# Index scores by four row groups, norm sums dealt between products, and another place for the inner parts

## The chip, the cores and the metric

The kernel runs on one NeuronCore of a Trainium2 chip. The metric is the device time of one execution in microseconds (us). Three runs of the kernel before gave 1913.39, 1914.81 and 1916.36, so the median is 1914.81 us.

## What is computed

The reference is two transformer blocks over 512 tokens of width 1024, in float32. The first block has two layers. Each takes an RMS norm, one wide projection that is split into 19 parts, four groups of heads (latent attention A, differential attention B, sparse attention C, a short convolution D), gates, and an output projection. The second block is a feed-forward (inner width 2816), a mixer with 16 heads, cross attention to 256 memory tokens, and a second feed-forward. What the change touches is this:

```python
# group C: which 128 keys a query may see
score = relu(einsum('bqhd,bkd->bqhk', qi, kidx))      # 8 index heads of 32
index = einsum('bqh,bqhk->bqk', wi, score) * idx_scale
_, sel = lax.top_k(index, topk)                       # topk = 128
# group A: latents are normed before they are projected up
q  = _rmsnorm(cq, qa_g) @ w_uq                        # cq 256 wide
kv = _rmsnorm(ckv, kva_g) @ w_ukv                     # ckv 128 wide
# second block
x = x + 0.5 * swiglu(rms_norm(x, g_ffn1), w_ffn1_gu, w_ffn1_down)
```

## The kernel before, in words

**Products.** Activations stand transposed, features on partitions: `hhi`, `hlo` (input of a projection, high and low part), 8 chunks of 512 tokens, 2048 bytes a chunk. Each float32 product is three fast ones (`products`, L859): input high by weight high, low by high, high by low. A *job* is one block of 128 output columns: 8 chunks of three products into one of two PSUM banks (`proj`), then evicted by DVE. Weights come by DMA in slots of a ring of four. For each slot ACT makes the high part (`make_high`, L1430), and POOL or DVE the low part (`make_low`, L652 or L1785): POOL for the jobs of a layer, DVE for the second block's feed-forward. A slot is prepared when the job two before it has ended.

**A layer.** The order of the work on PE is written out by hand: jobs QI0, QI1 (index queries), KI (index keys, copied four times over the partitions), KR, CQ0, then the four of `IDX_JOBS` (CQ1, CKV, BQ0, BK0), then VT0, the spreading of the latents' roots, and 34 steps of attention (L1072, L1084, L1108) that are filled with further jobs by a table. The output jobs OUT0 to OUT7 end the layer.

**Index scores.** There are 8 heads by 3 query blocks (the first block needs none), 24 units a layer. A query block sees 256, 384 or 512 keys, so that is the width of a unit. `idx_pair` (L951) does two units at once: for each of three passes (high by high, high by low, low by high) it issues one matmul of 32 rows for each of two heads, which stand on two different groups of 32 partitions, into `score[0]` and `score[1]`. A pair stands after chunks 0, 3 and 6 of each of the four jobs (`IDX_CHUNKS`), 12 pairs a layer. ACT takes each unit through relu into one of four buffers (L1529), DVE multiplies it by the head's weight and adds it to `index` (L1928, L1931). A pair waits until the relus of the pair before it are done.

**Topk.** 32 half rounds on DVE (`topk_half`: 8 largest values of three rows, or taking them out of the rows) find the 128 largest. The first four come before VT0 is evicted, the other 28 are dealt over the first 22 attention steps.

**Latent norm.** ACT squares the three latents (L1520), one in each of the first three jobs of `IDX_JOBS`. After BK0, PE sums the squares over partitions by 4 matmuls with one column for each latent (`add_squares`, L829; each shows as two instructions in the trace). DVE makes means, POOL the roots (L647), DVE diagonals of them (L1811), and PE spreads them over the partitions (`spread_roots`, L843). DVE then scales the latents (L1973) and takes the row minima of attention step 0 (L1829).

**Norm of a large input.** Products start on the unnormed input. In the first job, before chunk 6 (`SUM_CHUNK`), PE sums the squares; in the second, before chunk 4 (`SPREAD_CHUNK`), it spreads the roots into `turned[1]`; ACT copies that to `R` and DVE multiplies by it as it evicts. At the start of the second block (`N_FIRST`, `R_FIRST`) two norms are taken at once, so that there are twice the sums (16 matmuls, 32 instructions) and twice the spreads. There DVE computes the means, then the low part of job 1's weights, then the diagonals (after L2218); ACT copies `R` before it splits the weights of job 2, and DVE makes their low part after that.

**Feed-forward.** 44 up jobs make 22 inner chunks, which are kept as `inner_hi` and `inner_lo` in the arena (a block of SBUF that the stages share); 8 down jobs read them, 22 chunks each, 528 products in each feed-forward.

**Places in the arena**, from its start: the second mixer's `yhi2` at byte 0, the first block's `yhi` at byte 26624 (13 chunks of 2048), `inner_hi` at byte 19072 and `inner_lo` 22 chunks behind it.

## Time and profile before

| | |
|---|---|
| median of three runs | 1914.81 us |
| the profiled execution | 1912.63 us, span of its records 1910.8 us |
| granted clock of TensorE, mean | 0.991 |
| busy: PE, weight loads, DVE, ACT, POOL | 1872.0, 1473.2, 1036.4, 693.2, 385.9 us |
| products (L859), busy | the three forms with `hhi`/`hlo` 601.9 + 584.0 + 583.8 us |
| index scores (L961), matmuls | 144, in two stretches about 64 to 98 and 399 to 433 us |
| DMA | 26.4% of the engines' span |

The profile is of one execution; its times are from the first record. "Granted clock" is the share of full speed that TensorE's clock had. A row of a timeline gives the start, the busy time from first start to last end, the instruction, the tiles, the shape, how many were merged, and in brackets how long the engine had been idle and what released it. Matmuls overlap: the start-to-start time, not the busy time, is the pace.

### The profile page before, as it was taken

What the parts mean: (1) busy time and instruction counts of PE and PEld (TensorE: products, weight loads), DVE (VectorE), ACT (ScalarE), POOL (GpSimd) and SP (SyncE); (2) the same over time, 40 slices, a digit from 0 to 9 for tenths busy, and PEclk for the clock granted to TensorE, in tenths of its full rate; (3) what the DMA queues carried; (4) which work ended last, traced back from release to release, by engine and by line L of the source; (5) the groups of instructions that cost most, each with busy time, mean ns of one, the idle gap of its engine ahead of it and who ended that gap; (6) DMA issues with size and microseconds to landing.
All of it is one profiled execution on the core that took longest, in us unless ns stands there. A gap on an engine that the chain in (4) does not pass through costs nothing.

```text
span 1910.8 us, 26251 instructions
## 1 busy us (share of the span) xinstructions
PE 1872.0 (98%) x9284; PEld 1473.2 (77%) x9284; DVE 1036.4 (54%) x2106; ACT 693.2 (36%) x1274; POOL 385.9 (20%) x223
## 2 busy tenths in 40 slices
PE   6999999999999999999999999999999999999998
PEld 4666777866677788888888777777887888888887
DVE  4589787558978756455533323333544655555322
ACT  3344444434444443323222243343323432233222
POOL 2335252433524240000000122220110100000000
PEclk8999999999999999999999999999999999999999
DMA  5222112222211233223323412222221223333332
GB/s 188 67 67 78 56 56 79 90 67 67 77 57 56 79 128 98 89 98 99 99 99 99 151 53 78 69 83 82 88 89 45 68 90 96 99 99 97 101 99 88
DMA packets 48577, 165.65 MB, mean 87 GB/s; under 512 B 5592, under 2 KB 6104, under 8 KB 48472
## 3 DMA queue, kind: packets, MB, share of 16 engines
q1 hardware_dynamic: 47176, 161.88, 26.4%
q10 hardware_dynamic: 1296, 2.42, 0.4%
q8 instruction: 59, 0.97, 0.2%
q14 instruction: 46, 0.38, 0.1%
HBM read 162.12 MB, written 2.17 MB: 86 GB/s over the span
## 4 chain that ended last, share of the span: by engine, by line
PE 91%; DVE 4%; issue 2%; ACT 1%; DMA 1%; POOL 1%; DVEq 0%; POOLq 0%; SPq 0%; ACTq 0%
PE proj L859 73%; PE score L1072 2%; PE o L1108 2%; PE turned L1084 2%; PE proj L1226 1%; PE proj L1230 1%; PE turned L1294 1%; PE score L1288 1%; PE o L1318 1%; PE turned L829 1%; PE score L961 1%; PE o L1382 1%; PE score L1371 1%; DVE wlo L1785 1%; PE turned L843 1%
## 5 line engine op out<-in xcount | busy, mean ns | idle before, releaser
L859 PE MATMUL proj<-hhi,whi 128*128 128x512 f32 x1488 | 601.9, 405 | 5.5 <-POOL wlo L652 2.6
L859 PE MATMUL proj<-hlo,whi 128*128 128x512 f32 x1488 | 584.0, 392 | 0.0
L859 PE MATMUL proj<-hhi,wlo 128*128 128x512 f32 x1488 | 583.8, 392 | 0.0
L1430 ACT ACTIVATE whi<-ring 128x1024 fp32r<-128x1024 f32 x266 | 281.4, 1058 | 679.8 <-PE proj L859 633.3
L859 PEld LDWEIGHTS proj<-hhi,whi 128*128 128x128 f32 x1488 | 281.8, 189 | 103.4 <-issue 35.8
L859 PEld LDWEIGHTS proj<-hhi,wlo 128*128 128x128 f32 x1488 | 281.7, 189 | 61.0
L859 PEld LDWEIGHTS proj<-hlo,whi 128*128 128x128 f32 x1488 | 282.2, 190 | 55.7 <-issue 1.0
L1785 DVE TENSOR_TENSOR wlo<-ring,whi 128x1024 fp32r<-128x1024 f32 x187 | 228.5, 1222 | 165.4 <-ACT whi L1430 165.3
L652 POOL TENSOR_TENSOR wlo<-ring,whi 128x1024 fp32r<-128x1024 f32 x79 | 189.7, 2403 | 456.6 <-ACT whi L1430 456.4
L665 POOL TENSOR_TENSOR prob<-prob 128x512 f32<-128x512 f32 x30 | 46.4, 1547 | 859.2 <-ACT prob L1426 858.8
L1456 ACT ACTIVATE prob<-prob,negmax 128x256 f32<-128x256 f32 (+3 forms) x208 | 114.4, 551 | 153.6 <-DVE negmax L1829 153.6
L1829 DVE CUSTOM_DVE_ANT_0 prob<-score,arena 128x256 f32<-128x256 f32 (+3 forms) x208 | 93.1, 482 | 105.7 <-PE score L1288 81.7
L859 PE MATMUL proj<-inner_hi,wlo 128*128 128x512 f32 x352 | 139.0, 395 | 0.0
L859 PE MATMUL proj<-inner_hi,whi 128*128 128x512 f32 x352 | 139.0, 395 | 0.0
L859 PE MATMUL proj<-inner_lo,whi 128*128 128x512 f32 x352 | 139.0, 395 | 0.0
L859 PE MATMUL proj<-yhi,whi 128*128 128x512 f32 x256 | 101.0, 395 | 1.8 <-DVE wlo L1785 1.8
L859 PE MATMUL proj<-yhi,wlo 128*128 128x512 f32 x256 | 99.9, 390 | 0.0
L859 PE MATMUL proj<-ylo,whi 128*128 128x512 f32 x256 | 99.5, 389 | 0.0
L1857 DVE TENSOR_TENSOR tmp<-proj,R 128x512 f32<-128x512 f32 x48 | 33.2, 691 | 119.9 <-PE proj L859 114.0
L2178 DVE TENSOR_TENSOR tmp<-tmp,proj 128x512 f32<-128x512 f32 x44 | 30.3, 688 | 103.8 <-PE proj L859 103.6
L859 PEld LDWEIGHTS proj<-inner_lo,whi 128*128 128x128 f32 x352 | 66.1, 188 | 16.1
L859 PEld LDWEIGHTS proj<-inner_hi,whi 128*128 128x128 f32 x352 | 66.1, 188 | 16.1
(212 smaller groups left out, 2205.4 us busy)
## 6 DMA issues: line engine op xcount, KB each, us to landing
ring<-wstream SPq DMA_DIRECT2D x288, 512.0 KB, 3.5
arena<-lines SPq DMA_DIRECT2D x28, 256.0 KB, 5.7
arena<-x ACTq DMA_DIRECT2D x4, 512.0 KB, 6.3
out<-arena SPq DMA_DIRECT2D x8, 256.0 KB, 2.9
arena<-mem SPq DMA_DIRECT2D x1, 1024.0 KB, 8.4
par<-params ACTq DMA_DIRECT2D x3, 74.0 KB, 1.9
arena<-hot SPq DMA_DIRECT2D x2, 85.0 KB
arena<-rope SPq DMA_DIRECT2D x1, 128.0 KB, 6.6
```

Of the source, the lines that this page charges most:

```text
L652: pool.tensor_tensor(rounded(wlo[:, s, :]), ring[:, s, :], whi[:, h, :], ALU.subtract).then_inc(pool_lo_ready, 1)
L665: pool.tensor_tensor(sq[:, 3, :], sq[:, 0, :] if c == 1 else sq[:, 3, :], sq[:, c % 3, :], ALU.add)\
L859: mm = pe.matmul(b, rounded(w), rounded(rhs(v, k)), start=(first and n == 0 and p == 0), stop=(last and n == len(blocks) - 1 and p == 2))
L1072: pe.matmul(score[b][:, 0:W], lhsT, rhs, start=True, stop=True).then_inc(score_done, 1)
L1084: mm = pe.transpose(turned[g % 2][:, kb * P:(kb + 1) * P], prob[:, (2 * s + n) % 4, kb * P:(kb + 1) * P], ident[:, :])
L1108: mm = pe.matmul(opsum[o % 2][h * HD:(h + 1) * HD, qb * P:(qb + 1) * P], v, pT[:, (g - 1 + h) % 4, kb * P:(kb + 1) * P], start=(kb == 0), ...
L1430: act.activation(rounded(dst), src, ACT.Copy, scale=scale).then_inc(ready, 1)
L1456: act.activation(prob[:, i, 0:W], prob[:, i, 0:W], ACT.Exp, bias=negmax[:, i:i + 1], scale=-1.0, accum_out=rowsum[:, i:i + 1] if total is ...
L1785: dve.tensor_tensor(rounded(wlo[:, s, :]), ring[:, s, :], whi[:, h, :], ALU.subtract).then_inc(lo_ready, 1)
L1829: dve.tensor_tensor_reduce(prob[:, i, 0:W], src[:, 0:W], bias, 1.0, 3e38, ALU.add, ALU.min, negmax[:, i:i + 1]).then_inc(min_ready, 1)
L1857: return dve.tensor_tensor(dst, src, factors, ALU.mult)
L2178: dve.tensor_tensor(tmp[:, s, :], tmp[:, s, :], proj[(j + 1) % 2][:, :], ALU.mult)\
```

## The change

1. `idx_quad` takes the place of `idx_pair`. It issues four heads in each pass, one on each of the four groups of 32 partitions, into four banks: `score[0]`, `score[1]`, `opsum[0]`, `opsum[1]`. There are six quads a layer, after chunks 0 and 4 of CQ1, CKV and BQ0; BK0 has none. A quad waits for the relus of all four banks of the quad before it. The first one also waits until the index weights have left `opsum[0]`.
2. The latents' sums move into BK0: one latent's four matmuls after each of chunks 1, 3 and 5.
3. On DVE the mask of `index` and three topk halves move into BK0, ahead of its eviction; four more stand where four stood, and 25 instead of 28 are dealt over the attention steps.
4. At the start of the second block, the first norm's sums stay before chunk 6 and the second norm's move before chunk 7. The spreads move from before chunk 4 of the second job to before chunk 6.
5. `inner_hi` and `inner_lo` start at byte 18432 of the arena instead of 19072.

```diff
-IDX_CHUNKS = (0, 3, 6)
+IDX_AT = ((0, 0), (0, 4), (1, 0), (1, 4), (2, 0), (2, 4))
+LATENT_AT = ((3, 1), (3, 3), (3, 5))
...
-TOPK_EARLY = 4
+TOPK_FIRST, TOPK_EARLY = 3, 7
...
-        inner_at = (ARENA - 2 * FC * S) // 32 * 32
+        inner_at = B2_EARLY * S
...
+        idx_bank = (score[0], score[1], opsum[0], opsum[1])
...
+                def idx_quad(n):
                     if n == 0:
                         pe.wait_ge(idx_lo_ready, L * 3 + 3)
+                        pe.wait_ge(wi_copied, L + 1)
                     else:
                         pe.wait_ge(relu_ready, L * IDX_UNITS + n)
                     for p, (q, k) in enumerate(((idx_hi, idx_hi), (idx_hi, idx_lo), (idx_lo, idx_hi))):
-                        for i in range(2):
+                        for i in range(4):
                             h, qb = idx_unit(n + i)
-                            r = 32 * (h % 4)
-                            mm = pe.matmul(score[i][:, 0:width(qb)], ...
+                            r = 32 * i
+                            mm = pe.matmul(idx_bank[i][:, 0:width(qb)], ...
...
                     for k in range(KC):
                         in_chunk(name, k)
-                        if k in IDX_CHUNKS:
-                            idx_pair(2 * (len(IDX_CHUNKS) * n + IDX_CHUNKS.index(k)))
-
-                for c in range(3):
-                    pe.wait_ge(latsq_ready, L * 3 + (c + 1))
-                    mm = add_squares(turned[0], NT * (c // 2), sq[:, c, :], c == 0)
-                mm.then_inc(latsum_done, 1)
+                        if (n, k) in IDX_AT:
+                            idx_quad(4 * IDX_AT.index((n, k)))
+                        if (n, k) in LATENT_AT:
+                            c = LATENT_AT.index((n, k))
+                            pe.wait_ge(latsq_ready, L * 3 + (c + 1))
+                            mm = add_squares(turned[0], NT * (c // 2), sq[:, c, :], c == 0)
...
                     if k == SUM_CHUNK:
                         norm_sum(norm)
+                    if k == SUM_CHUNK + 1:
                         if norm == N_FIRST:
...
-                    if k == SPREAD_CHUNK:
+                    if k == (SPREAD_CHUNK if r != R_FIRST else SPREAD_CHUNK + 2):
...
+                    if not IDX_OF[i]:
+                        dve.wait_ge(idx_added, L * IDX_UNITS + IDX_UNITS)
+                        for qb in range(1, NQB):
+                            dve.memset(index[0:CHUNK, ...], -NEG).then_inc(topk_step, 1)
+                        for n in range(TOPK_FIRST):
+                            topk_half(n)
                     out_of(name, *early[name])
```

The order of PE's instructions, at three places. First job CQ1, behind chunk 0; `o` are the two banks `opsum`, and `REGISTER_ALU` works out what a wait compares with. Before:

```order
L954 REGISTER_ALU
L961 MATMUL score<-idx_hi 128x256
L961 MATMUL score<-idx_hi 128x384
L961 MATMUL score<-idx_lo,idx_hi 128x256
L961 MATMUL score<-idx_lo,idx_hi 128x384
L961 MATMUL score<-idx_hi,idx_lo 128x256
L961 MATMUL score<-idx_hi,idx_lo 128x384
L859 MATMUL proj<-hhi,whi 128x512
L859 MATMUL proj<-hlo,whi 128x512
L859 MATMUL proj<-hhi,wlo 128x512
L859 MATMUL proj<-hhi,whi 128x512
```

Now:

```order
L965 MATMUL score<-idx_hi 128x256
L965 MATMUL score<-idx_hi 128x384
L965 MATMUL o<-idx_hi 128x512
L965 MATMUL o<-idx_hi 128x256
L965 MATMUL score<-idx_lo,idx_hi 128x256
L965 MATMUL score<-idx_lo,idx_hi 128x384
L965 MATMUL o<-idx_lo,idx_hi 128x512
L965 MATMUL o<-idx_lo,idx_hi 128x256
L965 MATMUL score<-idx_hi,idx_lo 128x256
L965 MATMUL score<-idx_hi,idx_lo 128x384
L965 MATMUL o<-idx_hi,idx_lo 128x512
L965 MATMUL o<-idx_hi,idx_lo 128x256
```

The first two units have become four, in four banks, and the chunks that stood between two pairs come behind them.

Second, on PE, the end of job BK0 and the start of VT0; `turned<-ones,prob` are the latents' sums. Before:

```order
L961 MATMUL score<-idx_hi 128x384
L961 MATMUL score<-idx_hi 128x512
L961 MATMUL score<-idx_lo,idx_hi 128x384
L961 MATMUL score<-idx_lo,idx_hi 128x512
L961 MATMUL score<-idx_hi,idx_lo 128x384
L961 MATMUL score<-idx_hi,idx_lo 128x512
L859 MATMUL proj<-hhi,whi 128x512
L859 MATMUL proj<-hlo,whi 128x512
L859 MATMUL proj<-hhi,wlo 128x512
L829 MATMUL turned<-ones,prob 128x1 x4
L973 REGISTER_ALU
L829 MATMUL turned<-ones,prob 128x1 x8
```

Now, in the middle of BK0:

```order
L832 MATMUL turned<-ones,prob 128x1 x4
L862 MATMUL proj<-hhi,whi 128x512
L862 MATMUL proj<-hlo,whi 128x512
L862 MATMUL proj<-hhi,wlo 128x512
L862 MATMUL proj<-hhi,whi 128x512
L862 MATMUL proj<-hlo,whi 128x512
L862 MATMUL proj<-hhi,wlo 128x512
L977 REGISTER_ALU
L832 MATMUL turned<-ones,prob 128x1 x4
L862 MATMUL proj<-hhi,whi 128x512
L862 MATMUL proj<-hlo,whi 128x512
L862 MATMUL proj<-hhi,wlo 128x512
```

The last pair and the piece of three sums have left the end of BK0; the sums stand one by one, two chunks apart, within it.

Third, on PE, job 0 of the first feed-forward around its chunk 6; `turned<-ones` with `prob`, `pT` are the first norm's sums, with `tanh`, `tmp` the second's. Before:

```order
L859 MATMUL proj<-hhi,whi 128x512
L859 MATMUL proj<-hlo,whi 128x512
L859 MATMUL proj<-hhi,wlo 128x512
L829 MATMUL turned<-ones,prob 128x1 x4
L829 MATMUL turned<-ones,pT 128x1 x4
L829 MATMUL turned<-ones,tanh 128x1 x4
L829 MATMUL turned<-ones,tmp 128x1 x4
L859 MATMUL proj<-hhi,whi 128x512
L859 MATMUL proj<-hlo,whi 128x512
L859 MATMUL proj<-hhi,wlo 128x512
```

Now:

```order
L862 MATMUL proj<-hlo,whi 128x512
L862 MATMUL proj<-hhi,wlo 128x512
L832 MATMUL turned<-ones,prob 128x1 x4
L832 MATMUL turned<-ones,pT 128x1 x4
L862 MATMUL proj<-hhi,whi 128x512
L862 MATMUL proj<-hlo,whi 128x512
L862 MATMUL proj<-hhi,wlo 128x512
L832 MATMUL turned<-ones,tanh 128x1 x4
L832 MATMUL turned<-ones,tmp 128x1 x4
L862 MATMUL proj<-hhi,whi 128x512
L862 MATMUL proj<-hlo,whi 128x512
L862 MATMUL proj<-hhi,wlo 128x512
```

One chunk has come between the two norms' sums.

## Rows read from the trace of the kernel before

**Rows 1.** The page: the chain that ended last, by engine.
```profile
PE 91%; DVE 4%; issue 2%; ACT 1%; DMA 1%; POOL 1%; DVEq 0%; POOLq 0%; SPq 0%; ACTq 0%
```
**Rows 2.** Stretches: us, busy (x instructions) by engine, PEclk, DMA share, GB/s.
```profile
760.00:880.00 120.00, 120.00 (x531) 99.38 (x530) 60.97 (x77) 36.05 (x44) 0.00 (x0) 1.00 0.29 96
950.00:1070.00 120.00, 120.00 (x516) 96.50 (x515) 41.09 (x38) 33.13 (x37) 7.80 (x6) 1.00 0.31 101
1370.00:1390.00 20.00, 20.00 (x90) 16.57 (x89) 12.33 (x11) 8.47 (x12) 5.65 (x4) 1.00 0.27 85
335.00:363.00 28.00, 28.00 (x124) 22.94 (x123) 18.67 (x16) 14.03 (x20) 18.12 (x12) 1.00 0.31 95
```
**Rows 3.** Timeline of PE, layer 0, job BQ0: start us, us, instruction, count.
```profile
80.72 0.40 PE L859 MATMUL proj<-hhi,wlo 128*128 128x512 f32 x1
81.05 0.44 PE L961 MATMUL score<-idx_hi 32*128 32x256 f32 x2
...
82.11 0.39 PE L859 MATMUL proj<-hlo,whi 128*128 128x512 f32 x1
...
86.89 0.40 PE L859 MATMUL proj<-hhi,wlo 128*128 128x512 f32 x1
...
88.46 0.40 PE L859 MATMUL proj<-hlo,whi 128*128 128x512 f32 x1
```
**Rows 4.** Timeline of ACT, layer 0, job BQ0.
```profile
82.36 0.63 ACT L1520 ACTIVATE prob<-arena 128x512 f32<-128x512 f32 x1
85.04 0.87 ACT L1529 ACTIVATE arena<-score 128x512 f32<-128x512 f32 x2 [2.04 <-PE score L961]
88.04 0.98 ACT L1529 ACTIVATE arena<-score 128x384 f32<-128x384 f32 x2 [2.13 <-PE score L961]
```
**Rows 5.** Latent sums on PE's timeline; granted clock of two stretches.
```profile
97.54 2.74 PE L829 MATMUL turned<-ones,prob 128*128 128x1 f32 x24
...
100.92:104.29 3.37, 3.37 (x9) 2.61 (x8) 1.98 (x11) 0.00 (x0) 1.92 (x2) 0.51 0.00 0
35.35:39.70 4.35, 4.35 (x20) 3.35 (x20) 2.54 (x10) 0.00 (x0) 3.37 (x3) 1.00 0.69 217
```
**Rows 6.** Timelines behind job BK0 of layer 0: POOL, DVE, PE.
```profile
98.87 2.37 POOL L652 TENSOR_TENSOR wlo<-ring,whi 128x1024 fp32r<-128x1024 f32 x1 [6.21 <-ACT whi L1430]
101.19 1.65 POOL L647 TENSOR_TENSOR ms<-ms,mhalf 128x8 f32<-128x8 f32 x1
...
102.88 1.66 DVE L1811 TENSOR_SCALAR tmp<-ident,ms 128x128 f32<-128x128 f32 x8 [1.36 <-POOL ms L647]
...
113.38 0.29 DVE L1829 CUSTOM_DVE_ANT_0 prob<-score,arena 128x128 f32<-128x128 f32 x1
...
107.31 1.95 PE L843 MATMUL turned<-tmp,ones 128*128 128x128 f32 x16
109.18 0.49 PE L1072 MATMUL score<-arena 32*128 32x128 f32 x4
...
115.72 0.49 PE L1072 MATMUL score<-arena 32*128 32x128 f32 x4
```
**Rows 7.** Waits of PE: us in total, times, longest.
```profile
PE turned L1084 <- DVE prob L2012: 1.8, 2, 0.9
```
**Rows 8.** Timelines at the first feed-forward's start: PE, then DVE.
```profile
703.77 0.95 PE L829 MATMUL turned<-ones,prob 128*128 128x1 f32 x8
...
707.26 0.49 PE L859 MATMUL proj<-hhi,whi 128*128 128x512 f32 x1
...
709.15 0.77 PE L859 MATMUL proj<-hhi,whi 128*128 128x512 f32 x1
...
713.28 0.94 PE L843 MATMUL turned<-tmp,ones 128*128 128x128 f32 x7
...
707.78 1.22 DVE L1785 TENSOR_TENSOR wlo<-ring,whi 128x1024 fp32r<-128x1024 f32 x1
...
715.95 1.23 DVE L1785 TENSOR_TENSOR wlo<-ring,whi 128x1024 fp32r<-128x1024 f32 x1 [0.26 <-ACT whi L1430]
```

More of the change, by code:

```diff
@@ L191 @@
 IDX_UNITS = 8 * (NQB - 1)
-IDX_CHUNKS = (0, 3, 6)
+IDX_AT = ((0, 0), (0, 4), (1, 0), (1, 4), (2, 0), (2, 4))
+LATENT_AT = ((3, 1), (3, 3), (3, 5))
+IDX_OF = [[4 * m + g for m, (job, k) in enumerate(IDX_AT) if job == i for g in range(4)] for i in range(len(IDX_JOBS))]
 LAYER_SM, LAYER_GR, LAYER_PAIRS = 64, 48, 6
@@ L314, in idx_unit @@
 def idx_unit(n):
-    return 2 * (n // (2 * (NQB - 1))) + n % 2, n % (NQB - 1) + 1
+    return 4 * (n // (4 * (NQB - 1))) + n % 4, n % (NQB - 1) + 1
 def width(qb):
@@ L449, in build @@
         onat = view(NT, D)
-        inner_at = (ARENA - 2 * FC * S) // 32 * 32
-        assert inner_at >= B2_EARLY * S
+        inner_at = B2_EARLY * S
+        assert inner_at + 2 * FC * S <= ARENA
         inner_hi = over("inner_hi", "arena", [P, FC, S], inner_at)
@@ L948, in _ @@
                 in_job("CQ0", turn_w)
-                def idx_pair(n):
+                def idx_quad(n):
                     if n == 0:
                         pe.wait_ge(idx_lo_ready, L * 3 + 3)
+                        pe.wait_ge(wi_copied, L + 1)
                     else:
@@ L1522, in _ @@
                 for i, name in enumerate(IDX_JOBS):
-                    per = 2 * len(IDX_CHUNKS)
-                    for n in range(per * i, per * (i + 1)):
+                    for n in IDX_OF[i]:
                         qb = idx_unit(n)[1]
@@ L1528, in _ @@
                             act.wait_ge(idx_added, L * IDX_UNITS + (n - 3))
-                        act.activation(relu[:, n % 4, 0:width(qb)], score[n % 2][:, 0:width(qb)], ACT.Relu).then_inc(relu_ready, 1)
-                        if n == per * i + 1 and i < 3:
+                        act.activation(relu[:, n % 4, 0:width(qb)], idx_bank[n % 4][:, 0:width(qb)], ACT.Relu).then_inc(relu_ready, 1)
+                        if n == IDX_OF[i][1]:
                             square_latent(i)
@@ L1916, in _, with topk_half @@
                 b_scale = -(32 ** -0.5)
+                steps = 3 * (1 + TOPK_HALVES)
+                def topk_half(n):
+                    dve.wait_ge(topk_step, L * steps + (3 * n + 3))
+                    dve.memset(turnstile[:, 0:1], 0.0)
+                    for qb in range(1, NQB):
+                        row = index[:, qb - 1, 0:width(qb)]
+                        if n % 2 == 0:
+                            dve.max(m8[:, qb - 1, :], row).then_inc(topk_step, 1)
+                        else:
+                            dve.match_replace(row, m8[:, qb - 1, :], row, TAKEN).then_inc(topk_step, 1)
                 early = {"CQ1": (cqn[:, 1, :], 1.0), "CKV": (ckvn, 1.0), "BQ0": (bqT[:, 0, :], b_scale), "BK0": (bkT[:, 0, :], 1.0)}
@@ L1920, in _ @@
                 for i, name in enumerate(IDX_JOBS):
-                    per = 2 * len(IDX_CHUNKS)
-                    for n in range(per * i, per * (i + 1)):
+                    for n in IDX_OF[i]:
                         h, qb = idx_unit(n)
@@ L1932, in _ @@
                                                      ALU.mult, ALU.add).then_inc(idx_added, 1)
+                    if not IDX_OF[i]:
+                        dve.wait_ge(idx_added, L * IDX_UNITS + IDX_UNITS)
+                        for qb in range(1, NQB):
+                            dve.memset(index[0:CHUNK, qb - 1, width(qb) - CHUNK:width(qb)], -NEG).then_inc(topk_step, 1)
+                        for n in range(TOPK_FIRST):
+                            topk_half(n)
                     out_of(name, *early[name])
-                dve.wait_ge(idx_added, L * IDX_UNITS + IDX_UNITS)
-                for qb in range(1, NQB):
-                    dve.memset(index[0:CHUNK, qb - 1, width(qb) - CHUNK:width(qb)], -NEG).then_inc(topk_step, 1)
                 dve.wait_ge(latsum_done, L + 1)
@@ L1951, in stage_v @@
                     out_of(f"VT{n}", vstage[:, n % 2, :])
-                steps = 3 * (1 + TOPK_HALVES)
-                def topk_half(n):
-                    dve.wait_ge(topk_step, L * steps + (3 * n + 3))
-                    dve.memset(turnstile[:, 0:1], 0.0)
-                    for qb in range(1, NQB):
-                        row = index[:, qb - 1, 0:width(qb)]
-                        if n % 2 == 0:
-                            dve.max(m8[:, qb - 1, :], row).then_inc(topk_step, 1)
-                        else:
-                            dve.match_replace(row, m8[:, qb - 1, :], row, TAKEN).then_inc(topk_step, 1)
-                for n in range(TOPK_EARLY):
+                for n in range(TOPK_FIRST, TOPK_EARLY):
                     topk_half(n)
```

4 lines of the change are left out of this document (3 added, 1 removed).

## The prediction

> **What bounds the kernel now.** I read the chain of waits first: TensorE (PE) holds 91% of the chain that ended last [rows 1]. So a microsecond counts if it is PE's own, or a wait of PE; anything else is cover. I then read PE's timeline at the four places where the change touches it.
>
> The steady pace comes first. In the up projections 120 us hold 531 products, two of them cut by the edges: 120 / 529 = 0.2268 us each [rows 2]. Three make a chunk (0.68 us), 24 a job (5.44 us). The down projections, whose inputs are the inner parts, hold 516 in 120 us: 120 / 514 = 0.2335 us [rows 2].
>
> **Index scores.** What a pair costs PE is the time from the last product before it to the second one after it, less two steady products. Heads of 256 and 384 columns: 82.11 - 80.72 - 0.45 = 0.94 us. Heads of 384 and 512: 88.46 - 86.89 - 0.45 = 1.12 us [rows 3]. With 256, 384 and 512 columns at 2.4 GHz (0.107, 0.160, 0.213 us), both are 0.47 us plus three passes of the *wider* head. One after the other they would have cost 1.27 and 1.59. So two heads on two row groups already run side by side, and the third kind of pair (512, 256) is 1.11. Three pairs are 3.2 us, the twelve of a layer 12.7.
>
> A quad always holds a head of 512, so its least is 0.47 + 3 x 0.213 = 1.11 us. If only two groups can stream at once, it is 0.47 + 3 x (1536 / 2) / 2.4 GHz = 1.43 us (1536 is the mean of four widths). I take 1.15, near the least: the rows show no cost at all of the second stream, and 0.04 is left for the six extra weight loads. Six quads a layer: 6.9 us. The nine pairs that stood in jobs CQ1, CKV and BQ0 cost 9.5, so these three jobs end **2.6 us earlier** in each layer.
>
> Does the quad's wait for all four banks cost anything? The next quad comes four chunks later, 2.7 us. ACT needs 0.87 + 0.98 = 1.85 us for the widest four relus and 0.63 for a squared latent between them [rows 4]: 2.5 us. It fits, by 0.2 us. A miss would cost that much at three places a layer. Behind the relus, ACT's split of the next weights and POOL's low part (2.4 us) have a whole job (7.7 us) before PE needs them.
>
> **Latent sums.** Before, 24 one-column matmuls stand in one piece for 2.7 us, and a little later the granted clock is 0.51 for 3.4 us, the lower of its two levels, 1.2 GHz [rows 5]: eight whole products take 3.37 us there instead of 1.81, so 1.6 us are lost. The length of the piece seems to be the reason: behind the first norm's 16 in one piece the clock is full [rows 5]. Dealt in three pieces of 8 they cost the same 2.7 us, now in job BK0 in place of its three pairs (3.2): **0.45 us** less, and the clock should stay up.
>
> But what PE gains behind BK0 it meets again. Count from the end of BK0 (97.54). ACT splits slot BQ1, POOL makes its low part (98.87) and only then the root (101.19, ends at +5.3); DVE's diagonals end at +7.0 [rows 6]. Nothing of this chain moves: the sums are ready earlier, but POOL's queue puts the low part first. Before, PE came to the spreads at +9.8 and found all ready. Now it ends VT0 at +5.5 and **waits 1.5 us**. Spreads 1.9, step 0 6.5 (from 109.18 to 115.72 [rows 6]): it would issue the scores of step 1 at +15.4. Those need the row minima of step 0, which DVE gives at 113.4 to 113.9, +16.3 [rows 6]: four topk halves, the eviction of VT0 and the scaling of latents stand before them, as now. So PE waits another 0.9 and issues at +16.4 instead of +18.2: **1.8 us** a layer. Per layer 2.6 + 0.45 + 1.8 = 4.85, both 9.7 us; with quads of 1.43 it is 6.3, with 1.11 10.2.
>
> **Topk.** Three halves go from the attention steps to job BK0, where DVE waits for PE anyway (they end before BK0 does). DVE has 5 us less in the steps. PE waited 1.8 us in total for DVE's scaled rows [rows 7]; I take half, **0.9**, bounds 0 and 1.8. What is late next is PE's own work.
>
> **The first norm of the second block.** Before: sums from 703.77 to 707.26, then DVE computes the means and only then job 1's low part (707.78 to 709.00), so PE starts job 1 at 709.15, 1.9 after the sums; spreads at 713.28; job 2 needs DVE's low part at 715.95 to 717.18 [rows 8], 3.9 after the spreads' start, while PE takes 1.7 for the spreads and 2.7 for four chunks: no wait. The four chunks before the spreads took 4.13 us, not 2.72: the clock has fallen here too.
> Now: the second half of the sums ends one chunk later, at 4.2 us from the start of all; job 1 starts at 4.2 + 1.9 = 6.1, where PE was ready at 4.9: a wait of 1.2 instead of 0.4. Six chunks, 4.1. From the spreads on only two chunks cover DVE's 3.9: 1.7 + 1.4 = 3.1, so PE **waits about 0.9** for job 2's low part. Job 2 starts at 6.1 + 4.1 + 4.05 = 14.3 us, against 13.9 before: 0.3 slower even if the clock stays up, 1.7 if it falls as before (1.4 lost). Two pieces of 16 with one chunk between and a longer wait behind are hardly more work than before, so I expect it to fall: **1.5 us slower**, bounds 0.3 and 1.9.
>
> **Inner parts.** From the start of the arena they stood 9 chunks of 2048 bytes plus 640 bytes away, now exactly 9. That is all that sets the down products apart: same weights' place, same columns, full clock, DVE and ACT less busy than in the up projections [rows 2]. The output products of the second mixer read their high part from the arena's start, on the same grid: 90 in 20 us, 20 / 88.2 = 0.227 [rows 2], at full pace. Those of the first block read theirs 13 chunks into it: 124 in 28 us, 0.229 [rows 2], one of the three products slow. So the grid is likely the cause. 2 x 528 products x (0.2335 - 0.2268) = **7.0 us**. Bounds: 0 (the place doesn't matter) and 7.0; by the 0.229 row it would be 4.7. I take 7.0, since two of the three products there, and all of the second mixer's, are at full pace. Nothing covers this: PE never waits in the down projections.
>
> **Sum:** 9.7 + 0.9 - 1.5 + 7.0 = 16.1 us. The profiled execution took 1912.63, 2.2 under the median of the runs; the difference is taken off the median: 1914.81 - 16.1 = 1898.7, say **1899 us**.
>
> **The rivals.**
> *The grid does nothing* (26%). Against it: the pace of the second mixer's outputs. For it: the first block's outputs are on the grid and one product in three is as slow as in the down projections, so something else can slow a product. 1898.7 + 7.0 = 1905.7 us.
> *The clock falls at the new wait* (12%): 1.5 us idle, then spreads and short scores. For it: the clock fell after 2.7 us of thin work [rows 5]. Against: the idle time is shorter than that, and the spreads are matmuls of 128 columns, not of one. Costs 1.6 a layer: 1901.9 us. The Trainium skill, "TensorE: Matmul & The Clock Gate", section "HAM oscillation", says the same of gaps between bursts of matmuls: the engine comes back at half its clock; the 0.51 behind the thin sums agrees with it.
> *Four streams are slower than two* (11%). Between the bounds 1.11 and 1.43, a pass a third longer than 0.213 makes the quad 1.32 and takes 12 x 0.17 = 2.0 us off the gain: 1900.7 us. The same page, section "Measured speedup vs the span model", gives 3.07 times, not 4, for four row groups with 512 columns; by that a quad is 1.30 and the time 1900.5. No row of this trace has four groups.
> *Four groups do not run side by side at all* (4%), the one that ends slower: the heads stream in turn, a quad is 0.47 + 3 x 1536 / 2.4 GHz = 2.39 us. Six are 14.3 where nine pairs were 9.5: 4.8 lost, 2.25 won, 2.6 slower a layer; with the first norm's 1.5 and nothing from topk or grid 1914.8 + 5.1 + 1.5 = 1921.4 us. It decides from 1.83 us a quad. Against it: both kinds of pair.
> *The change hardly shows* (2%): quads at 1.43, clock falling in both layers, grid nothing: about 1912 us.
>
> **How the numbers follow.** The forecast keeps 45%. 0.2% (3.8 us) is about what a measurement of this kernel can tell from no change. Forecast and the first three rivals (94%) are all faster by more; I leave 1% of that for several misses at once: faster 0.93, same 0.04, slower 0.03. The range: down to 1895 (quads at 1.11, all of the topk wait gone, first norm only 0.3 slower: 0.5 + 0.9 + 1.2 better); up to 1909 (the grid does nothing and quads are 1.43: 1905.7 + 3.4).
>
> **What the profile of the change would show.** Pairs replaced by quads that cost 1.1 to 1.2 us by the same measure; granted clock 1.00 through VT0; a wait of about 1.5 us before the spreads put down to DVE's diagonals or POOL's root; about 516 - 531 in the 120 us windows of the down projections: 531 if the grid is right, 516 if not; waits of PE for DVE's low part near the start of jobs 1 and 2 of the first feed-forward, 1.2 and 0.9 us. I am wrong if quads exceed 1.4, if PE waits for relus by more than 0.3, or if the down products stay at 0.233.

## The result, and the profile after

Four runs of the changed kernel gave 1892.97 to 1897.44 us, median **1894.38 us**; four of the kernel before, taken beside them, 1914.72. The ratio is 0.990 (95% interval 0.9887 to 0.9912): 20.3 us faster. The forecast was 1899, its range 1895 to 1909: the sign is right, the gain was 4 us larger than the forecast 16.1, and the time lies 0.6 us below the range. The profiled execution took 1894.07 us, its span is 1892.3.

The page and PE's waits of the kernel after (us in total, times, longest); its line numbers are 3 to 8 higher, L862 is the products' L859 of before, L1090 is L1084:

```profile
PE 92%; DVE 3%; issue 2%; ACT 1%; POOL 1%; DMA 1%; POOLq 0%; DVEq 0%; SPq 0%; ACTq 0%
...
PE turned L846 <- DVE tmp L1817: 5.1, 2, 3.6
PE proj L862 <- DVE wlo L1791: 4.0, 10, 0.8
...
PE proj L992 <- ACT arena L1555: 0.4, 2, 0.2
...
PE score L1078 <- DVE negmax L1835: 0.8, 1, 0.8
```

Against [rows 7]: the wait for DVE's scaled rows (1.8 us) is gone, and a new one of 5.1 us stands before the spreads of the latents, 3.6 of it in one place. The forecast had 1.5 in each layer.

**Quads.** PE's timeline in layer 0, the first quad. Of its 12 matmuls only the first pass is shown, two heads in each row; the products stand before and behind it:

```profile
62.82 0.40 PE L862 MATMUL proj<-hhi,wlo 128*128 128x512 f32 x1
63.15 0.44 PE L965 MATMUL score<-idx_hi 32*128 32x256 f32 x2
63.16 0.50 PE L965 MATMUL o<-idx_hi 32*128 32x512 f32 x2
...
64.05 0.50 PE L862 MATMUL proj<-hhi,whi 128*128 128x512 f32 x1
64.39 0.39 PE L862 MATMUL proj<-hlo,whi 128*128 128x512 f32 x1
```

By the measure used for the pairs: 64.39 - 62.82 - 0.45 = 1.12 us; the second quad gives 1.10. That is the forecast's lower bound, 1.11: four heads cost what the widest costs alone. PE waits for no relu.

**Spreads of the latents**, POOL, DVE and PE of layer 0, then of layer 1:

```profile
94.95 2.40 POOL L655 TENSOR_TENSOR wlo<-ring,whi 128x1024 fp32r<-128x1024 f32 x1 [5.82 <-ACT whi L1437]
94.99 2.37 DVE L1963 TENSOR_TENSOR arena<-arena 128x1 f32<-128x1 f32 x1 [0.35 <-ACT arena L1540]
97.30 1.65 POOL L650 TENSOR_TENSOR ms<-ms,mhalf 128x8 f32<-128x8 f32 x1
97.46 0.16 DVE L1966 TENSOR_TENSOR arena<-arena,par 128x1 f32<-128x1 f32 x1
98.98 3.84 DVE L1817 TENSOR_SCALAR tmp<-ident,ms 128x128 f32<-128x128 f32 x8 [1.36 <-POOL ms L650]
100.40 2.34 POOL L655 TENSOR_TENSOR wlo<-ring,whi 128x1024 fp32r<-128x1024 f32 x1 [1.46 <-ACT whi L1437]
102.88 3.48 PE L846 MATMUL turned<-tmp,ones 128*128 128x128 f32 x16 [3.65 <-DVE tmp L1817]
...
430.60 1.66 DVE L1817 TENSOR_SCALAR tmp<-ident,ms 128x128 f32<-128x128 f32 x8 [1.35 <-POOL ms L650]
432.03 2.45 POOL L655 TENSOR_TENSOR wlo<-ring,whi 128x1024 fp32r<-128x1024 f32 x1 [1.47 <-ACT whi L1437]
432.31 2.05 PE L846 MATMUL turned<-tmp,ones 128*128 128x128 f32 x16 [1.45 <-DVE tmp L1817]
```

Look at where things end. DVE's subtraction of one column, 0.15 us elsewhere, ends at 97.36, POOL's low part at 97.35. The eight diagonals, 1.66 us before [rows 6], end at 102.82, right behind POOL's *next* low part (102.74). In layer 1 the same low part starts 1.43 us behind the diagonals' start, as in layer 0 (1.42), but there the eighth got in first. By the single records the eighth starts 0.06 us ahead of the low part in layer 1 and takes 0.28 us; in layer 0 it starts 0.04 us ahead and takes 2.46. So a few hundredths of a microsecond decide, but they decided alike in all seven kernels that keep this order: caught in layer 0, not in layer 1. In layer 0 PE therefore waits 3.65 us, and the granted clock falls (columns: us, PE busy and instructions, PEclk, DMA share, GB/s):

```profile
102.00:104.00 2.00, 1.12 (x6) 0.81 0.11 45
104.00:106.00 2.00, 2.00 (x12) 0.50 0.00 0
106.00:108.00 2.00, 2.00 (x11) 0.84 0.02 4
```

**First norm** of the second block, PE, then DVE, then the clock, and a down projection:

```profile
692.73 0.95 PE L832 MATMUL turned<-ones,prob 128*128 128x1 f32 x8
...
698.81 0.77 PE L862 MATMUL proj<-hhi,whi 128*128 128x512 f32 x1 [0.46 <-DVE wlo L1791]
...
707.86 0.47 PE L862 MATMUL proj<-hhi,whi 128*128 128x512 f32 x1 [0.72 <-DVE wlo L1791]
...
697.44 1.22 DVE L1791 TENSOR_TENSOR wlo<-ring,whi 128x1024 fp32r<-128x1024 f32 x1
```

```profile
698.00:700.00 2.00, 1.54 (x4) 0.50 0.82 250
...
930.00:1050.00 120.00, 120.00 (x531) 1.00 0.33 105
```

From the first sum to job 2: 707.86 - 692.73 = 15.13 us. Before, job 2 started at 717.83:

```profile
717.83 0.39 PE L859 MATMUL proj<-hhi,whi 128*128 128x512 f32 x1
```

That is 14.06. And 531 products stand in 120 us around the first down projection, where 516 stood [rows 2].

Where the 18.5 us of the profiled span went, from the same instructions in both timelines (the end of BK0's job is taken at ACT's exponential behind it, 98.70 and now 94.78 us in layer 0):

| stretch | forecast | measured |
|---|---|---|
| start, to the first index scores (63.78, now 63.15) | 0 | 0.6 |
| from there to the end of BK0's job, layer 0; layer 1 | 3.05; 3.05 | 3.3; 3.3 |
| from there to the scores of step 1 (17.0 in both layers; now 18.2; 15.25) | 1.8; 1.8 | -1.2; 1.7 |
| rest of the layer (topk) | 0.45; 0.45 | 1.65; 1.6 |
| first norm, to job 2 | -1.5 | -1.1 |
| both down projections | 7.0 | 7.0 |
| second mixer (the clock is 0.50 there for some 3 us less) | 0 | 1.6 |

### The profile page after: what moved, and what is told of

Same layout as the page of the kernel before. It is cut to its first block, busy times and chain, and to the rows that moved or that the text cites. A ratio compares the mean times of both kernels' runs of the same rounds, so it can differ in the third digit from the quotient of the medians.

```text
span 1892.3 us, 26241 instructions
## 1 busy us (share of the span) xinstructions
PE 1850.2 (98%) x9284; PEld 1466.0 (77%) x9284; DVE 1037.5 (55%) x2106; ACT 691.6 (37%) x1274; POOL 385.6 (20%) x223
## 4 chain that ended last, share of the span: by engine, by line
PE 92%; DVE 3%; issue 2%; ACT 1%; POOL 1%; DMA 1%; POOLq 0%; DVEq 0%; SPq 0%; ACTq 0%
PE proj L862 73%; PE score L1078 3%; PE o L1114 2%; PE turned L1090 2%; PE proj L1233 2%; PE proj L1237 1%; PE turned L1301 1%; PE score L1295 1%; PE o L1325 1%; PE turned L832 1%; DVE wlo L1791 1%; PE o L1389 1%; PE score L1378 1%; ACT whi L1437 1%; PE proj L992 1%
## 5 line engine op out<-in xcount | busy, mean ns | idle before, releaser
L862 PE MATMUL proj<-hhi,whi 128*128 128x512 f32 x1488 | 598.9, 403 | 6.7 <-POOL wlo L655 2.6
L862 PE MATMUL proj<-hhi,wlo 128*128 128x512 f32 x1488 | 582.1, 391 | 0.0
L862 PE MATMUL proj<-hlo,whi 128*128 128x512 f32 x1488 | 581.9, 391 | 0.0
L862 PEld LDWEIGHTS proj<-hhi,whi 128*128 128x128 f32 x1488 | 280.5, 189 | 101.0 <-issue 33.9
L862 PEld LDWEIGHTS proj<-hhi,wlo 128*128 128x128 f32 x1488 | 280.5, 189 | 60.1
L862 PEld LDWEIGHTS proj<-hlo,whi 128*128 128x128 f32 x1488 | 280.9, 189 | 56.0 <-issue 1.0
L862 PE MATMUL proj<-inner_hi,wlo 128*128 128x512 f32 x352 | 136.9, 389 | 0.0
L862 PE MATMUL proj<-inner_hi,whi 128*128 128x512 f32 x352 | 136.9, 389 | 0.0
L862 PE MATMUL proj<-inner_lo,whi 128*128 128x512 f32 x352 | 136.9, 389 | 0.0
L862 PE MATMUL proj<-yhi,whi 128*128 128x512 f32 x256 | 101.0, 394 | 1.8 <-DVE wlo L1791 1.8
L862 PE MATMUL proj<-yhi,wlo 128*128 128x512 f32 x256 | 99.9, 390 | 0.0
L862 PE MATMUL proj<-ylo,whi 128*128 128x512 f32 x256 | 99.5, 389 | 0.0
L862 PEld LDWEIGHTS proj<-inner_hi,whi 128*128 128x128 f32 x352 | 66.1, 188 | 13.8
L862 PEld LDWEIGHTS proj<-inner_hi,wlo 128*128 128x128 f32 x352 | 66.1, 188 | 13.8
```

The source lines that it names most:

```text
L862: mm = pe.matmul(b, rounded(w), rounded(rhs(v, k)), start=(first and n == 0 and p == 0), stop=(last and n == len(blocks) - 1 and p == 2))
```

## Experiments

Each is the changed kernel with one edit, unless it says otherwise. The kernel before was timed beside all of them (medians 1913.0 to 1913.7).

**The inner parts.** The kernel before, with nothing but their place changed:

```diff
-        inner_at = (ARENA - 2 * FC * S) // 32 * 32
+        inner_at = B2_EARLY * S
```

> The kernel before with one thing changed: the inner parts start 640 bytes earlier, 9 chunks of 2048 bytes from the arena's start. If the place sets the pace of the down products: 0.227 us each instead of 0.2335, the two down projections 3.5 us shorter each, the time 7.0 under the kernel before (about 1907.7), and every row ahead of the first down projection at the same time as before, within a start-up difference of some tenths. If the changed kernel's 0.227 comes from something else in it (other order on DVE or ACT): 0.2335 stays and the time stays.

1904.94 us, ratio 0.9958 (0.9941 to 0.9974). The stretch 930 to 1050 holds 531 products and 518 in the kernel before. From its first product to its last each of the two down projections takes 119.45 us, where the kernel before takes 122.96: 3.5 us less, twice. The term of 7.0 is the place's alone.

Is it the grid of 2048 bytes? Two other places, in words of 4 bytes:

```diff
+        inner_hi = over("inner_hi", "arena", [P, FC, S], inner_at + 32)
+        inner_lo = over("inner_lo", "arena", [P, FC, S], inner_at + FC * S + 128)
```

> The changed kernel with the inner high parts 128 bytes and the low parts 512 bytes off the grid of 2048 bytes. If any place off the grid costs, as the 640 bytes did, all three products of a chunk take 0.2335 and 120 us of a down projection hold 516: 7 us more, 1901.4. If only one of the two places costs, the high part's two products or the low part's one stand out, and the loss is 4.7 or 2.3 us. If what counted was the end of the arena (other tiles behind, not the grid), all stay at 0.2268 and the time at 1894.4.

```diff
-        inner_at = B2_EARLY * S
+        inner_at = B2_EARLY * S + 128
```

> The changed kernel with both inner parts 512 bytes off the grid, their distance from one another as in it. High part at 128 and low part at 512 bytes gave 527 products in 120 us, 640 bytes for both 518, the grid 531. If it is the distance between the two parts that made the 527: 531 here. If every place off the grid costs about the same small amount and 640 is worse by itself: about 527. If the loss grows with the distance from the grid: between 518 and 525.

The stretch 930 to 1050, first with high part +128 and low part +512 bytes, then with both +512:

```profile
930.00:1050.00 120.00, 120.00 (x527) 1.00 0.29 102
```

```profile
930.00:1050.00 120.00, 120.00 (x531) 1.00 0.32 104
```

Both at +512 keep the full pace (1893.72 us, two runs). So the grid of 2048 bytes is *not* what counts: 512 is enough. The places of 640 are 128 off that, and there all three products of a chunk take 0.233 us from start to start. With the high part alone at 128 the product of the high part by the high weights takes 0.232, that by the low weights 0.228, and the low part's 0.226: a down projection takes 120.63 us, 1.2 more than on the grid and not the 2.3 that two products of three at 0.2335 would cost. Why the two differ was not tried. (1897.29 us, of two runs that lie 7.6 apart, says less than the paces.)

The same three paces stand in the kernel before, in the first block's outputs: 0.232, 0.228 and 0.226 us. And there they have the same reason. The kernel's source puts `yhi` behind the bias (13 chunks), three chunks of index queries and keys *and* the 32 words of the index weights: byte 32896, 16 chunks and 128 bytes from the arena's start, not byte 26624. These outputs never were on the grid.

**The chain before the spreads.** POOL's low part kept away from the diagonals:

```diff
                 root(2 * NT)
+                pool.wait_ge(spread_ready, L * LAYER_ROOTS + (R_LATENT + 1))
                 prepare_after("VT0")
```

> The changed kernel, and POOL makes the low part behind VT0 only when DVE's eight diagonals are done. If the 3.65 us wait before the spreads of layer 0 comes from POOL's low part holding DVE off for the last diagonal: the diagonals take 1.66 us in both layers, PE waits 1.45 before the spreads in both, the granted clock stays 1.00 there and the sixteen spreads take 2.0 us instead of 3.5, step 1's scores of layer 0 come about 3.0 us sooner (layer 1 has 16.2 us from the end of BK0's job to them, layer 0 has 19.2), layer 1 stays as it is: about 1891.4 us. If something else delays the diagonals of layer 0, they still take 3.8 us and the time stays at 1894.4. If the clock falls for another reason than the long wait (the three thin pieces), the spreads are slow with the wait of 1.45 too, and about 1.3 us of the 3.0 are not won.

Layer 0 of this kernel, DVE, PE and the clock:

```profile
100.36 1.66 DVE L1818 TENSOR_SCALAR tmp<-ident,ms 128x128 f32<-128x128 f32 x8 [1.36 <-POOL ms L650]
...
102.07 2.05 PE L847 MATMUL turned<-tmp,ones 128*128 128x128 f32 x16 [1.47 <-DVE tmp L1818]
...
111.40 0.49 PE L1079 MATMUL score<-arena 32*128 32x128 f32 x4 [0.74 <-DVE negmax L1836]
```

```profile
62.00:64.00 2.00, 1.92 (x16) 0.97 0.65 256
64.00:66.00 2.00, 2.00 (x5) 0.50 0.02 4
...
102.00:104.00 2.00, 1.93 (x16) 1.00 0.61 238
```

Diagonals 1.66, wait 1.47, clock 1.00, spreads 2.05: all as expected. From the end of BK0's job to the scores of step 1 it is now 15.25 us, as in layer 1: 2.95 won. The collision is shown. So is what the clock fell behind: in all seven traces with the wait of 3.65 it fell to the lower level within the spreads or ahead of them, and at none of the nine places with a wait of 1.45 to 1.47. The time, 1892.45 us, is only 1.9 lower, where 3.0 was expected: in the profiled execution the clock fell at other places instead, behind the first quad of layer 0 (64:66) and of layer 1 (395), where it stayed at 1.00 in the changed kernel.

Sums in one piece again:

```diff
-                        if (n, k) in LATENT_AT:
-                            c = LATENT_AT.index((n, k))
-                            pe.wait_ge(latsq_ready, L * 3 + (c + 1))
-                            mm = add_squares(turned[0], NT * (c // 2), sq[:, c, :], c == 0)
...
+                for c in range(3):
+                    pe.wait_ge(latsq_ready, L * 3 + (c + 1))
+                    mm = add_squares(turned[0], NT * (c // 2), sq[:, c, :], c == 0)
```

> The changed kernel with the 24 sums of the latents in one piece behind BK0 again; quads and all the rest stay. The forecast's theory (dealing them keeps the clock up and costs less): the clock falls in VT0 in both layers, 1.6 us each, and the wait before the spreads goes, so 0.2 us a layer worse. The other theory, from the two traces: root and diagonals are tied to the end of BK0's job, which comes 2.8 us sooner when the sums stand behind it, and the job VT0 again covers the chain: PE waits for nothing before the spreads; in layer 0 the scores of step 1 come 3.7 us sooner, in layer 1 0.6 sooner: 1890 us. It would say that the dealing itself cost time as it is done here.

1889.86 us, **4.5 under the changed kernel** (its four runs, 1888.25 to 1891.88, all lie below that kernel's lowest). PE and the clock in layer 0:

```profile
91.03 2.73 PE L832 MATMUL turned<-ones,prob 128*128 128x1 f32 x24
100.81 1.95 PE L846 MATMUL turned<-tmp,ones 128*128 128x128 f32 x16
```

```profile
94.00:96.00 2.00, 2.00 (x6) 0.50 0.06 25
...
422.00:424.00 2.00, 2.00 (x6) 0.50 0.04 14
```

The clock does fall behind the thin piece, in both layers, as the forecast had it. But no wait stands before the spreads, and the scores of step 1 come 3.8 us sooner in layer 0 and 0.9 more in layer 1, where nothing collides. Dealing the sums, as the change does it, lost more than it saved: the forecast credited it with the clock and never weighed it against quads with the sums left in one piece.

The third way takes away what ties the chain to the end of the job:

```diff
-                for name in IDX_JOBS:
+                for name in IDX_JOBS[:-1]:
                     prepare_after(name)
                 pool.wait_ge(mean_ready, L * 2 + 2)
                 root(2 * NT)
+                pool.wait_ge(spread_ready, L * LAYER_ROOTS + (R_LATENT + 1))
+                prepare_after(IDX_JOBS[-1])
                 prepare_after("VT0")
...
                             topk_half(n)
+                        dve.wait_ge(latsum_done, L + 1)
+                        mean_squares(turned[0], ((0, 0, NT, 256), (NT, NT, NT, 128))).then_inc(mean_ready, 1)
                     out_of(name, *early[name])
-                dve.wait_ge(latsum_done, L + 1)
-                mean_squares(turned[0], ((0, 0, NT, 256), (NT, NT, NT, 128))).then_inc(mean_ready, 1)
+                spread_diag(L * LAYER_ROOTS + R_LATENT, spread[0], range(2 * NT)).then_inc(spread_ready, 1)
                 dve.wait_ge(lam_exp, L + 1)
...
-                spread_diag(L * LAYER_ROOTS + R_LATENT, spread[0], range(2 * NT)).then_inc(spread_ready, 1)
```

> The changed kernel, with the means of the latents taken by DVE before it evicts BK0, POOL's root before its low part behind BK0, and both of POOL's next low parts behind DVE's diagonals, which stand right behind the eviction. If PE's wait before the spreads is this chain's order: diagonals end about 3 us behind the end of BK0 and PE, there at +5.5, waits for nothing, clock 1.00; step 0 ends at +14, the row minima are there before it, so step 1's scores come 5 us sooner in layer 0 and 2 in layer 1: about 1887 us, 7 under the changed kernel. The rival: what is won is met again at the row minima of step 0 (0.8 us of wait now in layer 1) or at POOL's low part behind BK0, late by 1.6 us: then 1890 to 1891.

1886.99 us, ratio to before 0.9866 (0.9849 to 0.9882), 7.4 under the changed kernel. POOL, DVE and PE of layer 0:

```profile
92.40 1.65 POOL L650 TENSOR_TENSOR ms<-ms,mhalf 128x8 f32<-128x8 f32 x1 [3.48 <-DVE ms L1812]
95.94 2.39 POOL L655 TENSOR_TENSOR wlo<-ring,whi 128x1024 fp32r<-128x1024 f32 x1 [1.89 <-DVE tmp L1819]
...
94.21 1.65 DVE L1819 TENSOR_SCALAR tmp<-ident,ms 128x128 f32<-128x128 f32 x8
...
98.86 1.95 PE L848 MATMUL turned<-tmp,ones 128*128 128x128 f32 x16
```

The diagonals end 3 us before PE comes. The scores of step 1 stand 5.25 us earlier than in the changed kernel in layer 0 and 7.2 in layer 1 (two more there), as expected. PE still waits 0.4 us for the row minima, in both layers.

**Order in a quad.** The two loops exchanged:

```diff
-                    for p, (q, k) in enumerate(((idx_hi, idx_hi), (idx_hi, idx_lo), (idx_lo, idx_hi))):
-                        for i in range(4):
+                    for i in range(4):
+                        for p, (q, k) in enumerate(((idx_hi, idx_hi), (idx_hi, idx_lo), (idx_lo, idx_hi))):
```

> The changed kernel with the 12 matmuls of a quad issued head by head (three passes of a head in a row, on the same row group) in place of pass by pass. If a matmul can start beside its predecessor only when that is on another row group, and issue is in order: head i+1 starts beside head i's third pass, the three kinds of quad cost 0.47 + 1.28, 1.44 and 1.60 = 1.91 us on the mean in place of 1.11, 12 x 0.8 = 9.6 us more, 1904. If the four groups run side by side whatever the order, nothing changes. If they overlap only partly even in the changed kernel, the difference is smaller than 0.8 a quad.

1895.47 us (one run), and the second quad (behind the first the clock fell here, so that it can't be measured this way):

```profile
67.78 0.39 PE L862 MATMUL proj<-hhi,wlo 128*128 128x512 f32 x1
68.10 0.51 PE L965 MATMUL score<-idx_hi 32*128 32x384 f32 x2
68.12 0.45 PE L965 MATMUL o<-idx_hi 32*128 32x256 f32 x2
...
68.99 0.50 PE L862 MATMUL proj<-hhi,whi 128*128 128x512 f32 x1
69.33 0.39 PE L862 MATMUL proj<-hlo,whi 128*128 128x512 f32 x1
```

69.33 - 67.78 - 0.45 = 1.10: no difference. In layer 1 the whole stretch from the first quad to the end of BK0's job takes 31.72 us, in the changed kernel 31.62. My expectation of 1.91 a quad fell. The rows say why: the first passes of all four heads start within 0.03 us (68.10 to 68.13), though two further passes of a head are issued between each and the next. A pass that has to wait for its row group does not hold back the heads behind it.

**Topk.** `TOPK_FIRST, TOPK_EARLY = 3, 7` set to `0, 4`, so that none stands in BK0's job.

> The changed kernel with no topk half in BK0's job: four behind the diagonals as in the changed kernel, the other three in the attention steps again. If the topk relief is what the changed kernel won behind step 1 (1.65 us from the scores of step 1 to the end of the layer, in both layers): PE waits 0.9 us in each layer for DVE's scaled rows again and 1.6 us a layer are lost, 1897.7. If only the waits that the trace puts down to DVE count: 1.8 us, 1896.2. If DVE's load behind the steps doesn't matter: 1894.4.

1898.26 us (two runs, 1895.98 and 1900.53). Its waits of PE:

```profile
PE turned L1090 <- DVE prob L2020: 1.8, 2, 0.9
...
PE proj L992 <- ACT arena L1555: 1.2, 2, 0.6
```

In layer 0, from 113 to 200 us, it falls 1.7 us behind the changed kernel, over both layers 3.3. The recorded idle accounts for 2.6: 1.8, and 0.8 more than in the changed kernel at L992, which waits for ACT, itself behind DVE. Of the rest, 0.2 us a layer are lost as PE starts again behind the wait of 0.9: it costs 1.1. What the last 0.3 of both layers are was not followed.

**First norm.** One piece of 32 sums and spreads at chunk 4 again:

```diff
-                    if k == SUM_CHUNK + 1:
...
-                    if k == (SPREAD_CHUNK if r != R_FIRST else SPREAD_CHUNK + 2):
+                    if k == SPREAD_CHUNK:
```

> The changed kernel with the 32 sums of the first norm in one piece and the spreads at chunk 4 of job 1 again, all the rest as it is. The forecast's theory: from the first sum to job 2 14.0 us if the clock falls there and 13.1 if not, as in the two kernels without this edit, in place of 15.1 to 17.1 in the kernels with it: 1 to 3 us less, 1891 to 1893. If the edit costs nothing, the stretch stays at 15 or more.

From the first sum to job 2: 13.99 us, against 15.13, as expected. The time was to be 1891 to 1893; 1894.37 (two runs) cannot tell the 1.1. The low parts ahead:

```diff
+            make_low2(FFN1_AT + 1)
             dve.wait_ge(sumg_done, 1)
...
-            make_low2(FFN1_AT + 1)
             spread_diag(R_FIRST, spread[0], [*range(NT, 2 * NT), *range(NT)]).then_inc(spread_ready, 1)
+            make_low2(FFN1_AT + 2)
             dve.wait_ge(R_ready, DEPTH + 1)
```

(and ACT's split for job 2 ahead of its copy of the spreads.)

> The changed kernel, with DVE's low part for job 1 of the first feed-forward made before the sums of the first norm are waited for (DVE is idle there for 5.5 us), and ACT's and DVE's parts for job 2 before the wait for the spreads. If the two waits of PE (0.46 and 0.72 us) are only the place of these parts in DVE's and ACT's order, both go, the root takes 1.65 us instead of 2.56, and the time is 1.2 us lower. The clock still falls behind the four thin pieces (697 to 700.5), since nothing of PE's own work is changed; the rival is that the waits are part of what lowers it, and then up to 1.4 us more are won.

DVE and POOL of this kernel:

```profile
693.26 1.23 DVE L1795 TENSOR_TENSOR wlo<-ring,whi 128x1024 fp32r<-128x1024 f32 x1 [0.81 <-ACT whi L1437]
...
698.50 1.65 POOL L650 TENSOR_TENSOR ms<-ms,mhalf 128x8 f32<-128x8 f32 x1 [9.12 <-DVE ms L2234]
```

Both waits of PE are gone, the root takes 1.65 instead of 2.56 (it had run beside that low part), and the stretch is 12.24 us: 2.9 less, since the clock stayed up as well. In the next kernel, with the same order here, it fell, and the stretch is 13.84: a fall is worth 1.6. So the expectation that the clock falls there in any case was wrong for this execution. It is the fastest of four (1890.38); the median, 1894.29, did not move, where 1.2 us less were expected.

**Together.** The early root with the low parts ahead, and these two with the sums in one piece:

> The changed kernel with the edits of both earlier runs: root and diagonals of the latents early (5.7 and 7.2 us won at the scores of step 1 of the two layers), and the low parts ahead of the sums of the first norm (1.2 us). They touch different stretches, so they should add up: about 8.5 us under the changed kernel's 1894.4, 1886. If the clock's falls decide more than these waits do, it stays within 1 us of the 1887.0 of the early root alone.

> The changed kernel with root and diagonals of the latents early, the low parts ahead of the sums of the first norm, and these sums in one piece of 32 again, spreads two chunks sooner. From the first of the sums to job 2: 3.5 of sums, two chunks 1.4, job 1 5.4, spreads 1.7, no waits: 12.0 us, or 13 to 13.4 if the clock falls; the kernel with both edits and the dealt sums has 13.8. Time 1884 us, at most a microsecond under its 1885.0. If the dealt sums were worth having once the waits are gone, it is not under 1885.

1884.97 us (1883.23 to 1887.28; ratio to before 0.9852, 0.9834 to 0.9870) and 1886.85 (0.9860, 0.9843 to 0.9877). The stretch of the first norm is 13.84 and 13.83 us, with one fall of the clock in each: once the low parts are ahead, dealing these sums neither costs nor brings anything in these two traces. The two kernels beat the changed one by 9.4 and 7.5 us. Between them, and against the early root alone (1886.99), the runs can't choose.

## Why the prediction was right, and where it was not

**Inner parts: right in size, too narrow in cause.** 7.0 forecast, 7.0 measured, and shown by the place alone (3.5 in each down projection). But "exactly 9 chunks of 2048 bytes" was only one sufficient place; 512 bytes off is as good. And the rival of 26% was fed by a misreading. It took the first block's outputs to be on the grid; their high part starts 128 bytes off it, and their mean of 0.229 us is the 0.232, 0.228 and 0.226 of the run with the high part 128 bytes off, not one slow product of three. Read rightly, these rows were for the place and not against it.

**Quads: right.** 1.15 forecast, 1.11 measured, 0.24 us a layer: 3.3 instead of 3.05 up to BK0's end. The rivals of slower streams and of serial groups are out. The Trainium skill, "TensorE: Matmul & The Clock Gate", section "Measured speedup vs the span model", gives 3.07 times for four row groups with 512 columns. An estimate from that (a pass of 4 / 3.07 times the widest head's 0.213 us) makes a quad 1.30 us, and the trace does not agree: 1.12 and 1.10.

**Behind BK0: the step "nothing of this chain moves" failed in layer 0.** It held for the root (it starts 3.7 us behind BK0's end before and after), and in layer 1 for the diagonals too: a wait of 1.45, forecast 1.5, and 0.8 for the row minima, forecast 0.9, so 1.7 won of 1.8. In layer 0 the last diagonal met POOL's next low part. Before, that low part started 4 us after the diagonals had ended (at 104.54):

```profile
108.64 2.38 POOL L652 TENSOR_TENSOR wlo<-ring,whi 128x1024 fp32r<-128x1024 f32 x1 [5.79 <-ACT whi L1430]
```

It hangs on PE's end of VT0: the faster PE pulled it forward to 100.40, into them. The forecast had counted what POOL had queued ahead of the root, not what PE's early arrival would release behind it. It cost 2.2 us of wait and, with the clock, 2.9 in all. The Trainium skill, "SBUF — State Buffer", section "SBUF: two separate sides", says that DVE and GpSimd share a pair of ports, and that a DVE instruction with two inputs in SBUF (or in a mode that takes both ports) and a GpSimd instruction that reads SBUF exclude one another: the one that starts first holds the pair for its whole length. Beside POOL's low part the trace agrees (the one-column subtraction of 2.37 us). Beside POOL's root, which reads SBUF too, it does not: the one-column subtraction at 97.46, with both inputs in SBUF, took 0.16 us inside the root's 1.65.

**The rival "the clock falls at the new wait" came true, in layer 0 only**, where the wait was 3.65 and not 1.5. At 1.45 and 1.47 the clock stayed. The Trainium skill, "TensorE: Matmul & The Clock Gate", section "HAM oscillation", says that behind a long gap between bursts of matmuls the engine comes back at half its clock; the two lengths of wait agree. The fall behind the thin sums, which the prediction sets beside that section, is no such gap: PE is busy without a break there, and only the level (0.51) is the same.

**Topk: mis-sized.** 0.9 forecast, bounds 0 and 1.8; measured 3.3, outside them, and 3.3 again by the run that takes this part back. The upper bound was one line of the waits. It left out PE's waits for ACT, which is itself late behind DVE (0.8), and what a wait costs beyond its own length.

**First norm: right in sign, near in size** in this pair (1.1, forecast 1.5). Job 1 started 6.08 us behind the first sum, forecast 6.1; the spreads and the two chunks with their wait took 4.04, forecast 4.05 (the recorded idle of 0.72 counts from the end of the last product; by starts it is the 0.9 of the forecast). What was off is the fall of the clock: it stretched job 1's six chunks by 0.9 us and not by 1.4, since it began earlier and its first part lay under the wait for job 1, of which 0.46 was left as idle. Of seven other kernels with the same code here one took 15.1 us too, six 16.7 to 17.1, with a fall twice as long: the cost there is nearer 3.

**What nothing forecast:** 0.6 at the start and 1.6 in the second mixer, where the clock falls in both kernels but for a shorter time after. No edit touches these places; the kernel before and the same with the inner parts moved, which are alike up to there, have their first index scores at 63.78 and 62.53 us, so 0.6 is within what one kernel does.

The sum of 16.1 came near the 18.5 of the traces with errors that partly cancelled, which is luck: topk 2.4 too low, layer 0 behind BK0 3.0 too high, quads and first norm 0.9 too low, 2.2 unforecast. The other 1.8 of the 20.3 are the spread of the runs. And the lower end of the range, 1895, lies a microsecond below the prediction's own working: 1898.7 less 2.6 is 1896.1.

## What to carry to other kernels

When an engine on the path gets faster, look at every instruction that waits for *its* progress, and ask what these now run beside: here a low part moved 8 us forward into the eight diagonals it had always followed. To price a wait that goes, add up all waits that hang on the same late engine, through the others too. And tie a short chain that the path waits for (mean, root, diagonals) to its own data, not to the end of the job it happens to stand in.

## What the hardware showed unexpectedly

- A TENSOR_TENSOR or TENSOR_SCALAR of DVE with its inputs in SBUF that comes behind the start of POOL's low part (a TENSOR_TENSOR of 128x1024) does not run until that has ended. In eleven kernels one column took 2.31 to 2.37 us instead of 0.15, and its end met the end of the low part. Not held were MAX8 and MATCH_REPLACE8, instructions with one input in PSUM (17 ran inside low parts in the changed kernel, an eviction in its 0.69 us), and what stood beside POOL's root of 128x8 (0.16 us for the one column).
- The granted clock falls behind thin or interrupted PE work. Two places were alike in every trace: it fell behind the 24 latent sums in one piece (six of six, three kernels by two layers), never behind three pieces of 8, and behind the wait of 3.65 us (seven of seven). Others were not: in the changed kernel it stayed up behind the first quads, in two others it was at 0.50 for 3 to 4 us behind the same quads; behind the first norm's 32 sums in one piece it fell in the kernel before and not in the same kernel with the inner parts moved; the start (22 to 32 us) fell in the kernel before and not in the changed one. One fall of 3 to 4 us costs 1.4 to 1.6, one of twice that 3.2 in the second mixer. Runs of one kernel lie 1 to 8 us apart, and falls are part of it, not all: the two runs of the first other place have a mean granted clock of 0.995 (1893.5 us) and 0.990 (1901.1), but of the changed kernel's runs the fastest has 0.992 and the slowest 0.993. So an edit worth 1 to 2 us is read from the stretch it touches, not from the median.
- Four row groups run wholly side by side, in either order of issue: 1.10 to 1.12 us a quad both ways.
- The place of a product's moving operand in SBUF sets its pace: 0.2267 us where both parts stand 0 or 512 bytes off the 2048 grid (counted from the arena's start), 0.2335 where both stand 640 off, and 0.232 and 0.228 for the two products of a high part that stands 128 off beside a low part at full pace. Other distances were not tried.
